# A two-model forward pass on one core: norms' roots behind the feed-forward products, attention halves split earlier, other POOL and load order

## The chip, the core and the metric

The kernel is one program on one core of a Trainium2 chip. The metric is device time in microseconds, the median of several runs. One further execution was recorded by the hardware profiler. Five engines work side by side: PE (matmul), DVE, ACT, POOL and SP, which here only issues DMAs.

## What is computed

Two blocks run in a row over 256 tokens of width 1024 (with 16 extra "meta" tokens in the second, so 272 columns there). The first has an mLSTM and sparse-attention layer and an HGRN2 layer, each behind an RMS norm. The second is a feed-forward, a mixer (stick-breaking attention beside an RWKV-7 recurrence), and a second feed-forward:

```python
def rms_norm_2(x, g):
    xf = x.astype(jnp.float32)
    y = xf * lax.rsqrt(jnp.mean(xf * xf, axis=-1, keepdims=True) + RMS_EPS)
    return (y * g.astype(jnp.float32)).astype(x.dtype)

def swiglu(h, w_gate, w_up, w_down):
    return (jax.nn.silu(h @ w_gate) * (h @ w_up)) @ w_down
...
        n = rms_norm_2(h, ffn1_norm[l])
        h = h + 0.5 * swiglu(n, ffn1_w_gate[l], ffn1_w_up[l], ffn1_w_down[l])
        n = rms_norm_2(h, mix_norm[l])
        proj = n @ w_in[l]
        ...
        h = h + jnp.concatenate([sb_out, rw_out], axis=-1) @ w_out[l]
        n = rms_norm_2(h, ffn2_norm[l])
        h = h + 0.5 * swiglu(n, ffn2_w_gate[l], ffn2_w_up[l], ffn2_w_down[l])
    return rms_norm_2(h, final_norm)[:, N_META:]
```

The root in `rms_norm_2` is one number per token, so it commutes with `h @ w_gate` and `h @ w_up`.

## The kernel before

**Layout.** Activations lie with features on the 128 partitions and tokens along the row: `xT` (the running sum), `hT` and `mixT` hold 8 tiles of 272 columns. All weights are cut into 253 units of 128x1024 numbers (512 KB) in one stream, in the order of use: `U_E` and `U_C` (first projection), `U_EO` (its output), `U_H` and `U_HO` (HGRN), `U_F1` (44 gate and up units in turn, then 22 down units), `U_P` and `U_PO` (mixer), `U_F2`. SP loads them into a ring of `SLOTS = 4`.

**Split products.** Every number of a large product is split into a rounded high half and the remainder. For a weight unit ACT writes `whi` (`high`, L1463) and POOL subtracts it from the ring to write `wlo` (`low`, L602); only then is the ring slot free for SP's next load. Activations get `aH` (ACT) and `aL` (DVE). PE makes three matmuls of each pair (`mm3`): high by high, high by low, low by high. A unit is 24 matmuls. Results go to four PSUM banks in turn (`MM_BANKS`); PE writes a bank again only when DVE or ACT has read the last result (`drained_v`, `drained_a`).

**Order.** Each engine runs its own program in the written order, with semaphores between them. ACT's `ahead(u)` waits until PE has used unit `u` and then makes the high half of unit `u + 4`. Where `ahead` stands behind another ACT step, a late input of that step delays the weights too. POOL's `lows(u0, u1)` makes the low halves of a range of units; between the ranges stand the decays of HGRN and `inverse_starts`, which fills `rGI` with identities and masks `rN` for the block inversion in RWKV.

**A norm.** `residual` (DVE, L1843) adds each of the 8 output tiles to `xT`. ACT squares a tile (`square`, L1402), DVE adds the first `SUMMED = 5` squares (L1834). PE sums over the partitions with a matrix of ones, ACT forms the root with Ln and Exp (`rstd`), DVE forms `hT` = x times weight times root (L1866), ACT rounds it to `aH`, DVE writes the remainder `aL` (L1872), and the first unit of the next projection can start. Meanwhile PE multiplies constants in `filler`.

**Feed-forward.** ACT takes the tanh of a gate bank (`fth`, L1673). DVE's `pair` makes `fhalf` from it and the gate (L2172), the product with the up bank (`fact`, L2177), and its two halves `fH` (L2180) and `fL` (L2182).

**The first layer's end.** `project_halves` multiplies the two halves of the output projection separately: attention's four tiles first (`mix_split` 1 to 4), the four memory heads' after them. All splits are written after the last memory head.

## Time and profile before

| | us |
|---|---|
| median of 3 runs | 1084.57 |
| the 3 runs | 1083.26 to 1085.09 |
| profiled execution, its own time | 1077.73 |
| span in its profile | 1075.9 |
| busy in it: PE, POOL, ACT, DVE | 992.6, 654.8, 535.2, 533.0 |
| mean granted TensorE clock | 0.974 of full speed |

Busy times are sums over the whole span. Which engine matters where is read from what PE waits for at one place, and from the time stamps around it. The profiled execution's own time is 6.8 us below the median of the three runs.

### The profile page before, as it was taken

The page shows a single profiled execution, that of the slowest core. Times are in us where ns is not written, and L with a number is a line of the kernel's source. Part 1 is how long each engine was busy: PE and PEld are TensorE (multiplying, and loading weights), DVE is VectorE, ACT ScalarE, POOL GpSimd, SP SyncE. Part 2 cuts the span into 40 slices and gives each one's busy share as a digit, 9 for nine tenths or more (in the row PEclk, how much of TensorE's full clock was granted, in tenths as well). Part 3 has the DMA queues.
Part 4 walks back from the last instruction along what each step waited for, and adds up shares of the span by engine and source line. Part 5 has one row for each costly group of instructions (what it writes and reads, how often), then busy time and mean ns, then how long its engine had stood idle before and what let it go on. Part 6 is the DMA issues. An engine that isn't in the chain of part 4 may idle for free.

```text
span 1075.9 us, 22914 instructions
## 1 busy us (share of the span) xinstructions
PE 992.6 (92%) x9068; PEld 944.6 (88%) x9068; DVE 533.0 (50%) x735; ACT 535.2 (50%) x765; POOL 654.8 (61%) x271
## 2 busy tenths in 40 slices
PE   5998999799799778999999999999999999999996
PEld 5987777698799767899999998999898879999996
DVE  4346424654410895586662003375274668777301
ACT  6565564556554445644444436676331554444441
POOL 2785234356689731698787775554620269888882
PEclk9998999999899899999999999999899999999999
DMA  8553122133355200455555553333300046555551
GB/s 321 195 169 106 60 79 98 59 118 128 127 177 177 79 1 2 149 187 177 177 171 177 176 176 124 117 117 115 99 4 4 23 136 207 188 192 179 192 177 41
DMA packets 38993, 139.79 MB, mean 130 GB/s; under 512 B 4224, under 2 KB 5504, under 8 KB 38784
## 3 DMA queue, kind: packets, MB, share of 16 engines
...
## 4 chain that ended last, share of the span: by engine, by line
PE 55%; issue 21%; POOL 12%; DVE 8%; ACT 2%; DMA 1%; SPq 0%; POOLq 0%; DVEq 0%; ACTq 0%
PE ps L667 55%; POOL wlo L602 11%; DVE qkl L1834 3%; DVE hA L2133 1%; DVE hT L1866 1%; ACT whi L1463 1%; ACT dif L1402 1%; DMA ring<-in_stream 1%; DVE sq L1834 0%; ACT rstd L1402 0%; POOL dif L626 0%; PE ps L1208 0%; DVE hA L1834 0%; DVE rGI L1834 0%; DVE aL L1872 0%
## 5 line engine op out<-in xcount | busy, mean ns | idle before, releaser
L602 POOL TENSOR_TENSOR wlo<-ring,whi 128x1024 fp32r<-128x1024 f32 x251 | 611.8, 2455 | 372.4 <-ACT whi L1463 371.5
L667 PE MATMUL ps<-aH,whi 128*128 128x256 f32 (+1 forms) x1528 | 444.0, 291 | 27.5 <-DVE aL L1834 11.8
L667 PE MATMUL ps<-aH,wlo 128*128 128x256 f32 (+1 forms) x1528 | 438.2, 287 | 0.0
L667 PE MATMUL ps<-aL,whi 128*128 128x256 f32 (+1 forms) x1528 | 437.8, 287 | 0.0
L1463 ACT ACTIVATE whi<-ring 128x1024 fp32r<-128x1024 f32 x253 | 266.3, 1058 | 122.9 <-PE ps L667 107.3
L667 PEld LDWEIGHTS ps<-aH,whi 128*128 128x128 f32 x1528 | 293.4, 192 | 35.3 <-POOL wlo L602 17.6
L667 PEld LDWEIGHTS ps<-aL,whi 128*128 128x128 f32 x1528 | 292.8, 192 | 0.5 <-issue 0.4
L667 PEld LDWEIGHTS ps<-aH,wlo 128*128 128x128 f32 x1528 | 293.1, 192 | 0.0
L667 PE MATMUL ps<-fH,wlo 128*128 128x272 f32 (+1 forms) x352 | 100.8, 286 | 0.0
L667 PE MATMUL ps<-fH,whi 128*128 128x272 f32 (+1 forms) x352 | 100.4, 285 | 0.0
L667 PE MATMUL ps<-fL,whi 128*128 128x272 f32 (+1 forms) x352 | 100.4, 285 | 0.0
L2182 DVE TENSOR_TENSOR fL<-fact,fH 128x272 f32 (+3 forms) x44 | 97.3, 2212 | 5.1
L1843 DVE SCALAR_TENSOR_TENSOR xT<-ps,xT 128x256 f32<-128x256 f32 (+1 forms) x40 | 17.1, 428 | 124.8 <-PE ps L667 124.1
L667 PEld LDWEIGHTS ps<-fH,whi 128*128 128x128 f32 x352 | 66.5, 189 | 0.0
L667 PEld LDWEIGHTS ps<-fL,whi 128*128 128x128 f32 x352 | 66.3, 188 | 0.0
L667 PEld LDWEIGHTS ps<-fH,wlo 128*128 128x128 f32 x352 | 66.2, 188 | 0.0
L1402 ACT ACTIVATE sq<-xT 128x256 f32<-128x256 f32 (+1 forms) x48 | 20.2, 421 | 69.7 <-DVE xT L1843 66.9
L1673 ACT ACTIVATE fth<-ps 128x272 f32<-128x272 f32 (+1 forms) x44 | 17.2, 391 | 60.8 <-PE ps L667 60.7
L667 PE MATMUL ps<-qkl 128*128 128x128 f32 x240 | 33.7, 307 | 13.2 <-DVE qkl L1834 13.2
L2180 DVE CAST fH<-fact 128x272 f32 (+3 forms) x44 | 42.4, 963 | 6.3 <-DVE fact L2177 3.4
L667 PEld LDWEIGHTS ps<-qkl 128*128 128x128 f32 x240 | 32.1, 219 | 14.7 <-DVE qkl L1834 14.7
L2177 DVE TENSOR_TENSOR fact<-fhalf,ps 128x272 f32<-128x272 f32 (+1 forms) x44 | 18.9, 430 | 37.2 <-PE ps L667 35.6
...
## 6 DMA issues: line engine op xcount, KB each, us to landing
ring<-in_stream SPq DMA_DIRECT2D x253, 512.0 KB, 3.3
...
out<-hT SPq DMA_DIRECT2D x1, 1024.0 KB, 4.6
...
```

Of the source, the lines that this page charges most:

```text
L602: nc.gpsimd.tensor_tensor(wlo[:, s, :], ring[:, s, :], whi[:, s, :].bitcast(F32), ALU.subtract).then_inc(S("w_split"), 1)
L667: return nc.tensor.matmul(out, lhsT, rhs, start=start, stop=stop, skip_group_check=True)
L1402: step(nc.scalar.activation(out, in_, f, **kw), sem)
L1463: nc.scalar.activation(whi[:, v % SLOTS, :], ring[:, v % SLOTS, :], ACT.Copy).then_inc(S("w_high"), 1)
L1673: nc.scalar.activation(fth[:, f4, c0:TT], ps[:, (g0 + 2 * f4) % MM_BANKS, 0:TT - c0], ACT.Tanh, scale=0.5).then_inc(S("ffn_th"), 1)
L1834: step(nc.vector.tensor_tensor(out, a, b, op), sem)
L1843: step(nc.vector.scalar_tensor_tensor(out=out, in0=a, scalar=s, in1=b, op0=op0, op1=op1), sem)
L1866: nc.vector.scalar_tensor_tensor(out=hT[:, j, c0:c0 + n], in0=xT[:, j, c0:c0 + n], scalar=V(w, j), in1=rstd[:, 0:n], op0=ALU.mult, op1=ALU ...
L2133: step(nc.vector.copy_predicated(v(out, 4), m.bitcast(U32), v(src, 4)), "lev_a")
L2177: nc.vector.tensor_tensor(prod, half, ps[:, (g0 + 2 * f4 + 1) % MM_BANKS, 0:TT - c0], ALU.mult).then_inc(S("drained_v"), 1)
L2180: nc.vector.tensor_copy(fH[:, f, c0:TT], prod).then_inc(S("ffn_hi"), 1)
L2182: nc.vector.tensor_tensor(fL[:, f, c0:TT], prod, fH[:, f, c0:TT].bitcast(F32), ALU.subtract).then_inc(S("ffn_split"), 1)
```

## The change

In words:

- **Late roots.** Before both feed-forwards (`LATE`), the input is split without the root: ACT writes `fxH` = x times norm weight, rounded, in front of the square; DVE writes `fxL` (`low_half`) from the sum itself. PE multiplies the first two units, and only then sums the squares. DVE multiplies each gate bank with the root before the tanh, and each of the 8 outputs of the down projection before adding it. The pair `fxH`, `fxL` takes the memory of `hT`, `mixT`.
- **Attention split earlier.** The four attention tiles are split by ACT behind unit 31 and by DVE behind unit 32 of the first projection, among the memory heads.
- **RWKV.** POOL fills the identities before the low halves of the four units `U_PO` to `U_PO` + 3, which wait for RWKV's third `r_u`. On PE three of the four key transposes stand before and within the products `r_u`.
- **Start.** DVE adds seven squares, PE multiplies two matrices for the first norm rather than four; ACT makes one high half before the root and one behind it; DVE's low halves follow, the second one within the norm.
- **End.** The output goes out in four pieces. `residual` adds its squares behind the sums, not ahead of them. `SUMMED` is a number per norm.

The diff, cut:

```diff
+LATE = ("ffn1", "ffn2")
+SUMMED = {"norm0": 7, "norm1": 5, "ffn1": 7, "mix": 5, "ffn2": 5, "final": 5}
+
+
+def sums_up_to(tag):
+
+    return sum(SUMMED[n] - 1 for n in NORMS[:NORMS.index(tag) + 1])
...
-        hT = sb("hT", [P, KT, TT])
-        mixT = sb("mixT", [P, KT, TT])
+        own = ExitStack()
+        hT = sb("hT", [P, KT, TT], at=own)
+        mixT = sb("mixT", [P, KT, TT], at=own)
+        own.close()
+        fxH = sb("fxH", [P, KT, TT], F32R)
+        fxL = sb("fxL", [P, KT, TT], F32R)
...
+        def acts(tag):
+
+            return (fxH[:], fxL[:]) if tag in ("ffn1", "ffn2") else (aH[:], aL[:])
...
-            sp.wait_ge(S("norm_h"), len(NORMS) * KT)
-            sp.dma_start(out_d, hT[:, :, TM:TT]).then_inc(S("out_done"), 16)
-            sp.wait_ge(S("out_done"), 16)
+            for k in range(0, KT, 2):
+                sp.wait_ge(S("norm_h"), (len(NORMS) - 1) * KT + k + 2)
+                sp.dma_start(out_d[:, k:k + 2, :], hT[:, k:k + 2, TM:TT]).then_inc(S("out_done"), 16)
+            sp.wait_ge(S("out_done"), 16 * KT // 2)
...
-            lows(U_HO + SLOTS, U_PO + SLOTS)
+            lows(U_HO + SLOTS, U_PO)
             inverse_starts()
-            lows(U_PO + SLOTS, N_UNITS)
+            pool.wait_ge(S("r_u"), 3)
+            lows(U_PO, N_UNITS)
...
                 i = NORMS.index(tag)
                 if i == 0:
                     pe.wait_ge(S("early_in"), 32)
-                else:
+                elif tag not in LATE:
                     filler(1)
-                pe.wait_ge(S("norm_sum"), (SUMMED - 1) * (i + 1))
-                mm(ps[:, 7, 0:n], C("ones"), sq[:, 0, 0:n], True, False)
-                for k in range(SUMMED, KT):
+                pe.wait_ge(S("norm_sum"), sums_up_to(tag))
+                m = mm(ps[:, 7, 0:n], C("ones"), sq[:, 0, 0:n], True, SUMMED[tag] == KT)
+                for k in range(SUMMED[tag], KT):
                     pe.wait_ge(S("norm_sq"), KT * i + k + 1)
                     m = mm(ps[:, 7, 0:n], C("ones"), sq[:, k, 0:n], False, k == KT - 1)
                 m.then_inc(S("norm_ss"), 1)
-                if i and tag != "final":
+                if tag in ("norm1", "mix"):
...
-                feature_pair(u0, g0, c0, ("norm_h", NORMS.index(tag) * KT))
+                feature_pair(u0, g0, c0, ("norm_h", NORMS.index(tag) * KT), tag)
+                norm(tag, TT - c0)
...
+                turned(6, key(0, 0)).then_inc(S("r_tok"), 1)
                 pe.wait_ge(S("r_wc"), 3)
                 for g, b in ((0, 0), (1, 4)):
                     pe.wait_ge(S("r_g"), level_count(last_level(g), g))
+                    if g == 1:
+                        turned(2, key(0, 1)).then_inc(S("r_tok"), 1)
+                        turned(3, key(1, 0)).then_inc(S("r_tok"), 1)
...
-                turned(2, key(0, 0)).then_inc(S("r_tok"), 1)
-                turned(3, key(0, 1)).then_inc(S("r_tok"), 1)
-                turned(6, key(1, 0)).then_inc(S("r_tok"), 1)
                 pe.wait_ge(S("r_tokb"), 1)
-                turned(2, key(1, 1)).then_inc(S("r_tok"), 1)
+                turned(6, key(1, 1)).then_inc(S("r_tok"), 1)
 
                 for c in range(4):
                     p, e = c // 2, c % 2
                     if e == 0:
-                        pe.wait_ge(S("r_tokb"), (4, 4)[p])
+                        pe.wait_ge(S("r_tokb"), (3, 4)[p])
...
+                if tag in LATE:
+                    func(acts(tag)[0][:, k, c0:TT], xT[:, k, c0:TT], ACT.Identity, "norm_hi", scale=V(tag, k))
                 func(sq[:, k, 0:n], xT[:, k, c0:c0 + n], ACT.Square, "norm_sq")
 
             def norm(tag, n):
                 act.wait_ge(S("norm_ss"), NORMS.index(tag) + 1)
                 func(rstd[:, 0:n], ps[:, 7, 0:n], ACT.Ln, scale=1.0 / D, bias=eps[:, 0:1])
                 func(rstd[:, 0:n], rstd[:, 0:n], ACT.Exp, "norm_rstd", scale=-0.5)
-                if tag != "final":
+                if tag == "norm0":
+                    high(1)
+                if tag in ("norm0", "norm1", "mix"):
                     for k in range(KT):
-                        act.wait_ge(S("norm_x"), NORMS.index(tag) * KT + k + 1)
+                        act.wait_ge(S("norm_x"), ("norm0", "norm1", "mix").index(tag) * KT + k + 1)
...
-                for u in range(2):
-                    high(u)
+                high(0)
                 act.wait_ge(S("setup"), 5)
-                act.wait_ge(S("early_in"), 32)
...
+                if tag in LATE:
+                    ahead(u0 + n_units - 1)
...
+                    if j == 31:
+                        act.wait_ge(S("att_o"), 8)
+                        for n in range(4):
+                            func(fxH[:, 4 + n, TM:TT], mixT[:, 4 + n, TM:TT], ACT.Copy, "mix_hi")
 
             def memory_out():
-                for n in range(4):
-                    act.wait_ge(S("mix_x"), n + 1)
-                    func(aH[:, 4 + n, TM:TT], mixT[:, 4 + n, TM:TT], ACT.Copy, "mix_hi")
...
-                    act.wait_ge(S("w_used"), it * 8 + (u0 + 2 * f4 + 1))
+                    ahead(u0 + 2 * f4, it)
+                    act.wait_ge(S("ffn_gate"), it * 4 + (first + f4 + 1))
...
+            def low(u):
+                dve.wait_ge(S("w_high"), u + 1)
+                tt(wlo[:, u, :], ring[:, u, :], whi[:, u, :].bitcast(F32), ALU.subtract, "w_split")
+
             def norm(tag, c0, n, w):
 
                 i = NORMS.index(tag) * KT
-                if tag == "norm0":
-                    for k in range(1, SUMMED):
+                first = tag == "norm0"
+                if first:
...
-                    for u in range(2):
-                        dve.wait_ge(S("w_high"), u + 1)
-                        tt(wlo[:, u, :], ring[:, u, :], whi[:, u, :].bitcast(F32), ALU.subtract, "w_split")
-                if tag == "norm0":
                     dve.wait_ge(S("early_in"), 32)
                     scaled_vectors()
+                    low(0)
...
+                lag = 1 if first else 2
...
+                    if first and j == 1:
+                        low(1)
+                    if split and j >= lag:
+                        k = j - lag
...
+                    if j == 32:
+                        for n in range(4):
+                            at = mixT[:, 4 + n, TM:TT]
+                            dve.wait_ge(S("mix_hi"), n + 1)
+                            tt(fxL[:, 4 + n, TM:TT], at, fxH[:, 4 + n, TM:TT].bitcast(F32), ALU.subtract, "mix_split")
...
             def residual(tag, g0, c0, scale=1.0):
-                for m in range(KT):
-                    if 2 <= m <= SUMMED:
-                        add_square(tag, m - 1, TT if tag in ("ffn1", "mix") else T)
-                    dve.wait_ge(S("w_used"), used_by(g0 + m))
-                    out = ps[:, (g0 + m // 2) % MM_BANKS, (m % 2) * T:(m % 2 + 1) * T] if tag in ("norm1", "ffn2") else \
-                        ps[:, (g0 + m) % MM_BANKS, 0:TT - c0]
-                    stt(xT[:, m, c0:TT], out, scale, xT[:, m, c0:TT], ALU.mult, ALU.add, "drained_v")
+                wide = TT if tag in ("ffn1", "mix") else T
+                for m in range(KT + 1):
+                    if m < KT:
+                        dve.wait_ge(S("w_used"), used_by(g0 + m))
+                        out = ps[:, (g0 + m // 2) % MM_BANKS, (m % 2) * T:(m % 2 + 1) * T] if tag in ("norm1", "ffn2") else \
+                            ps[:, (g0 + m) % MM_BANKS, 0:TT - c0]
+                        if tag in ("mix", "final"):
+                            tt(out, out, rstd[:, 0:TT - c0], ALU.mult)
+                        stt(xT[:, m, c0:TT], out, scale, xT[:, m, c0:TT], ALU.mult, ALU.add, "drained_v")
+                    if tag in LATE and m >= 1:
+                        low_half(tag, m - 1, wide)
+                    if 2 <= m <= SUMMED[tag]:
+                        add_square(tag, m - 1, wide)
+                if tag in LATE:
+                    dve.wait_ge(S("norm_rstd"), NORMS.index(tag) + 1)
+
+            def low_half(tag, k, n):
+
+                high, low = [t[:, k, TT - n:TT] for t in acts(tag)]
+                dve.wait_ge(S("norm_hi"), NORMS.index(tag) * KT + k + 1)
+                stt(low, xT[:, k, TT - n:TT], V(tag, k), high.bitcast(F32), ALU.mult, ALU.subtract, "norm_h")
...
+                    gate = ps[:, (g0 + 2 * f4) % MM_BANKS, 0:TT - c0]
+                    dve.wait_ge(S("w_used"), it * 8 + (u0 + 2 * f4 + 1))
+                    nc.vector.tensor_tensor(gate, gate, rstd[:, 0:TT - c0], ALU.mult).then_inc(S("ffn_gate"), 1)
                     dve.wait_ge(S("ffn_th"), it * 4 + (first + f4 + 1))
                     dve.wait_ge(S("drained_v"), it * 8 + (d0 + 2 * f4))
                     nc.vector.scalar_tensor_tensor(out=half, in0=fth[:, f4, c0:TT], scalar=1.0,
-                                                   in1=ps[:, (g0 + 2 * f4) % MM_BANKS, 0:TT - c0], op0=ALU.add,
+                                                   in1=gate, op0=ALU.add,
```

How it moves instructions, at three places. DVE, from the first residual of the HGRN output projection to the first feed-forward, before (`xT` is the sum, `sq` the squares):

```order
L1843 SCALAR_TENSOR_TENSOR xT<-ps,xT 128x256 [waits w_used,mix_split]
L1843 SCALAR_TENSOR_TENSOR xT<-ps,xT 128x256 [waits w_used,drained_v]
L1834 TENSOR_TENSOR sq<-sq 128x272 [waits norm_sq,drained_v]
L1843 SCALAR_TENSOR_TENSOR xT<-ps,xT 128x256 [waits w_used,norm_sum]
L1834 TENSOR_TENSOR sq<-sq 128x272 [waits norm_sq,drained_v]
L1843 SCALAR_TENSOR_TENSOR xT<-ps,xT 128x256 [waits w_used,norm_sum]
```

and in the changed kernel, the same place:

```order
L1867 SCALAR_TENSOR_TENSOR xT<-ps,xT 128x256 [waits w_used,mix_split]
L1867 SCALAR_TENSOR_TENSOR xT<-ps,xT 128x256 [waits w_used,drained_v]
L1867 SCALAR_TENSOR_TENSOR fxL<-xT,vec,fxH 128x272 [waits norm_hi,drained_v]
L1867 SCALAR_TENSOR_TENSOR xT<-ps,xT 128x256 [waits w_used,norm_h]
L1867 SCALAR_TENSOR_TENSOR fxL<-xT,vec,fxH 128x272 [waits norm_hi,drained_v]
L1858 TENSOR_TENSOR sq<-sq 128x272 [waits norm_sq,norm_h]
L1867 SCALAR_TENSOR_TENSOR xT<-ps,xT 128x256 [waits w_used,norm_sum]
```

Each later tile now has two instructions with two SBUF inputs (`fxL`, `sq`) behind its sum, where it had one.

ACT, at the end of the first projection, before (`hm` is the memory heads' output, `mixT` attention's, the `th` row the output gates' tanh):

```order
L1402 ACTIVATE rs<-hm 128x1024 [waits mlstm_h,mlstm_d]
L1402 ACTIVATE sq<-ps,vec 128x256 [waits w_used,ScalarE_once]
L1463 ACTIVATE whi<-ring 128x1024 [waits w_ready2,w_used,drained_a]
L1402 ACTIVATE aH<-mixT 128x256 [waits mix_x]
L1402 ACTIVATE aH<-mixT 128x256 [waits mix_x,mix_hi] x3
L1402 ACT_TABLE_LOAD [waits qk_ready]
L1402 ACTIVATE th<-sq 128x2048 [waits mix_hi]
```

and now:

```order
L1420 ACTIVATE fxH<-mixT 128x256 [waits att_o,mlstm_e]
L1420 ACTIVATE fxH<-mixT 128x256 [waits mix_hi] x3
L1420 ACTIVATE sq<-ps,vec 128x256 [waits w_used,mix_hi]
L1486 ACTIVATE whi<-ring 128x1024 [waits w_ready0,w_used,drained_a]
L1420 ACTIVATE mad<-ps 128x256 [waits mlstm_h,mlstm_o]
L1420 ACTIVATE mem<-ps 128x256 [waits mlstm_st,mlstm_s,mlstm_d]
```

The four copies stand two memory heads earlier, and the tanh follows directly on the last weight unit.

PE in RWKV, behind the last inversion level, before (`ps<-cst,sq` are the key transposes, `ps<-rWA,rGI` the products `r_u`):

```order
L667 MATMUL ps<-rWA,rGI 64x128 [waits r_g,r_wc]
L667 MATMUL ps<-rWA,rGI 64x128 x15
L667 MATMUL ps<-rWA,rGI 64x128 [waits r_g]
L667 MATMUL ps<-rWA,rGI 64x128 x17
L1208 MATMUL ps<-cst,sq 128x128 x12
L1208 MATMUL ps<-cst,sq 128x128 [waits r_tokb]
L1208 MATMUL ps<-cst,sq 128x128 x3
L667 MATMUL ps<-rWA,rN 64x64 [waits r_uc,r_tokb]
```

and now:

```order
L1227 MATMUL ps<-cst,sq 128x128 x4
L683 MATMUL ps<-rWA,rGI 64x128 [waits r_g,r_wc]
L683 MATMUL ps<-rWA,rGI 64x128 x15
L1227 MATMUL ps<-cst,sq 128x128 [waits r_g]
L1227 MATMUL ps<-cst,sq 128x128 x7
L683 MATMUL ps<-rWA,rGI 64x128 x18
L1227 MATMUL ps<-cst,sq 128x128 [waits r_tokb]
L1227 MATMUL ps<-cst,sq 128x128 x3
L683 MATMUL ps<-rWA,rN 64x64 [waits r_uc,r_tokb]
```

Twelve of the sixteen transposes moved ahead of the last products; one group of four stands between them and the state products.

## Rows read from the trace of the kernel before

**Rows 1.** The page: busy times, share of the span, instructions.

```profile
PE 992.6 (92%) x9068; PEld 944.6 (88%) x9068; DVE 533.0 (50%) x735; ACT 535.2 (50%) x765; POOL 654.8 (61%) x271
```

**Rows 2.** The chain in order of time: start us, us, what; both feed-forwards.

```profile
447.62 202.93 PE ps L667 x1594
...
876.14 190.37 PE ps L667 x1594
```

**Rows 3.** Timeline of PE, start (first two), first layer's end, FFN 1 entrance.

```profile
7.56 3.78 PE L667 MATMUL ps<-sq,cst 128*128 128x256 f32 x8 [7.56 <-DMA cst<-in_cst]
15.89 0.55 PE L667 MATMUL ps<-aH,whi 128*128 128x256 f32 x1 [4.55 <-DVE aL L1872]
214.50 0.55 PE L667 MATMUL ps<-aH,whi 128*128 128x256 f32 x1 [7.52 <-DVE aL L1834]
...
441.92 0.89 PE L667 MATMUL ps<-cst 128*128 128x432 f32 x2
447.62 0.36 PE L667 MATMUL ps<-aH,whi 128*128 128x272 f32 x1 [0.81 <-DVE aL L1872]
```

**Rows 4.** Timeline there, then windows (PE, PEld, DVE, ACT, POOL, PEclk, DMA).

```profile
211.56 1.74 ACT L1402 ACTIVATE aH<-mixT 128x256 fp32r<-128x256 f32 x4
211.99 3.74 DVE L1834 TENSOR_TENSOR aL<-mixT,aH 128x256 fp32r<-128x256 f32 x4 [3.08 <-ACT aH L1402]
225.19 0.42 DVE L1834 TENSOR_TENSOR aL<-ps,aH 128x256 fp32r<-128x256 f32 x1 [1.04 <-ACT aH L1402]
240.55 0.89 PE L667 MATMUL ps<-cst 128*128 128x432 f32 x2
...
214.50:220.00 5.50, 5.50 (x29) 5.39 (x30) 4.43 (x6) 4.14 (x4) 0.00 (x0) 0.68 0.29 98
```

**Rows 5.** DVE beside POOL: FFN 2's loop, then the entrance of FFN 1.

```profile
928.16 1.89 DVE L2180 CAST fH<-fact 128x256 f32 x1 [0.16 <-DVE fact L2177]
927.50 9.76 POOL L602 TENSOR_TENSOR wlo<-ring,whi 128x1024 fp32r<-128x1024 f32 x4 [2.07 <-ACT whi L1463]
435.70 1.54 DVE L1834 TENSOR_TENSOR sq<-sq 128x272 f32<-128x272 f32 x1 [0.57 <-ACT sq L1402]
426.85 17.33 POOL L602 TENSOR_TENSOR wlo<-ring,whi 128x1024 fp32r<-128x1024 f32 x7 [33.76 <-ACT whi L1463]
```

**Rows 6.** Groups of DVE by form: busy us, mean ns, idle before.

```profile
L2182 DVE TENSOR_TENSOR fL<-fact,fH 128x256 f32 x20 | 49.3, 2464 | 2.5
L1872 DVE TENSOR_TENSOR aL<-hT,aH 128x272 fp32r<-128x272 f32 x16 | 6.6, 435 | 0.0
L2177 DVE TENSOR_TENSOR fact<-fhalf,ps 128x256 f32<-128x256 f32 x22 | 9.3, 422 | 13.2 <-PE ps L667 12.1
```

**Rows 7.** Timeline at the entrance of FFN 2.

```profile
868.13 0.89 PE L667 MATMUL ps<-cst 128*128 128x432 f32 x2
872.10 1.15 PE L667 MATMUL ps<-sq,cst 128*128 128x256 f32 x4 [0.70 <-ACT sq L1402]
```

**Rows 8.** Timeline of RWKV's start, then windows.

```profile
763.81 0.38 ACT L1402 ACTIVATE mixT<-ps 128x272 f32<-128x272 f32 x1
770.45 2.13 POOL L639 COPY rGI<-cst 128x1088 f32<-128x1088 f32 x2
773.61 5.60 PE L667 MATMUL ps<-hT,sq 64*64 64x128 f32 x64 [2.44 <-DVE rA L1834]
...
776.00:778.00 2.00, 2.00 (x30) 2.00 (x24) 1.77 (x3) 0.00 (x0) 1.99 (x1) 0.50 0.01 4
```

**Rows 9.** Timeline: state products in RWKV, the end; the page's DMA issue.

```profile
821.82 0.34 PE L667 MATMUL ps<-rWA,rN 64*64 64x64 f32 x4 [1.52 <-DVE rN L2318]
848.66 2.40 POOL L602 TENSOR_TENSOR wlo<-ring,whi 128x1024 fp32r<-128x1024 f32 x1 [46.54 <-ACT whi L1463]
1067.62 3.26 DVE L1866 SCALAR_TENSOR_TENSOR hT<-xT,vec,rstd 128x256 f32<-128x256 f32 x8 [3.05 <-ACT rstd L1402]
...
out<-hT SPq DMA_DIRECT2D x1, 1024.0 KB, 4.6
```

32 lines of the change are left out of this document (13 added, 19 removed).

## The prediction, made before the changed kernel was run

> **What bounds the kernel now.** I read the busy times of the page first: PE is busy 992.6 of 1075.9 us, POOL 654.8, ACT and DVE 535 each [rows 1]. So no other engine bounds the whole, and the part to be won is the 83 us in which PE stands or multiplies for nothing. The chain of waits says where PE cannot be helped: 1594 matmuls of the first feed-forward in 202.93 us (0.127 each, so a unit of 24 is 3.06 and a gate and up pair 6.1), and as many of the second in 190.37 us (0.119, 2.87 and 5.7) [rows 2]. The change takes no weight unit away. Then I read PE's timeline for gaps at the places that the diff touches: the start (first product at 15.89), 7.52 us at the first layer's end, 5.7 us from the last product before FFN 1 (441.92) to its first (447.62) [rows 3], 8.0 us before FFN 2 (868.13 to 876.14) [rows 2, 7], 2.44 us and half the clock at RWKV's start [rows 8], 1.52 us in its state products, and the end behind the last norm [rows 9]. That is about 27 us in reach. Last I read what DVE and POOL do to each other, since the change gives DVE more work at these places.
>
> DVE instructions that read PSUM cost the same with POOL at work or not: `fact` takes 422 ns in the mean of 22 [rows 6]. Those with two SBUF inputs don't: a remainder of 256 columns takes 0.435 when POOL rests, 2.464 in the mean in the feed-forward, the square's sum 1.54 instead of 0.43 while POOL runs seven low halves in a row (17.33, so 2.48 each), and even the cast `fH` 1.89 beside four of them [rows 5, 6]. They wait until POOL's running instruction is through.
>
> The Trainium skill has this as a rule (SBUF — State Buffer, section "Who interferes with whom"): DVE and GpSimd share one port pair as an exclusive lock, which a DVE instruction takes when both its inputs lie in SBUF, and the later one fully blocks. This case's trace agrees, 2.464 against 0.435. The rule speaks against this change, since `fxL` is made from `xT` and `fxH`, both in SBUF, at the moment when POOL is busiest. Without it the two entrances would be worth 11.1 us, with it the 5.4 below.
>
> **The change part by part.** Gains in us, against the profiled execution (1077.73, of which the span is 1075.9).
>
> *Start, 0.7.* Eight records in 3.78 are four matmuls at 0.94 [rows 3]; two go, but DVE adds two more squares (0.43 each), so the root comes about 1.1 earlier. PE's first product could gain 1.3, but the second high half now stands behind the root, and the later loads hang on it. Bounds 0 and 1.3; I take the middle.
>
> *First layer's end, 4.5.* ACT's four copies (1.74) and DVE's four remainders (3.74) leave the path [rows 4]; PE's 7.52 go almost whole, so attention's half starts at about 207.0, not 214.50. It takes 96 matmuls, some 11 us. But the memory heads' half hangs on its own chain (tanh, Ln, Exp, first `aL` at 225.19 [rows 4]), which gains only the 1.74 of the copies and about 1 that ACT waited for PE's sums: first `aL` at 222.4, last at 225. PE then waits 4 us between the halves, and ends at 235.5 instead of 240.55 [rows 4]. The slow clock behind the gap (0.68 in the window from 214.50 [rows 4]) goes or comes back behind the new one, so 4.5. Lower bound 3 (the clock falls again), upper 8 (the whole gap and the clock).
>
> *Entrance of FFN 1, 3.0.* The root leaves the path; two matmuls over the squares (two take 1.15 with the tail of the second, or 0.46 and 0.46 when others follow them [rows 7]) follow the pair: nothing waiting, 5.7 - 0.9 = 4.8. What is late next is DVE. Behind the last output it has a sum (0.42), two remainders and a square's sum, each of the latter 1.5 with POOL busy [rows 5]: done at 442.2 + 0.4 + 3.0 = 445.6. The first unit touches the last tile 2.5 us after its start, so PE starts at 443.2, and ACT, which now has two steps per tile and the highs of weights behind them, adds about 0.4: PE waits 1.7 instead of 5.7, less 0.9: 3.0. Bounds 4.6 (remainders at 0.435) and 0.8 (at 2.464).
>
> *Entrance of FFN 2, 2.4.* Here four matmuls stand behind the pair, 1.6. When the last output is done (868.13) DVE has three tiles left: 868.6 + 3 x (0.45 + 1.5) = 874.4, less 2.5: PE starts at 872.0, a wait of 3.9. 8.0 - 3.9 - 1.6 = 2.5, I say 2.4. Bounds 6.3 (no wait) and 0 (remainders at 2.464 give 874.8, and the 1.6 eat the rest).
>
> *Roots on outputs, -1.0.* Each down output gets a product of 0.42 in front of its sum, by `fact`'s row [rows 6]. For seven tiles PE's next output covers it; for the last it lies on the path to the norm, twice: 0.9 to 1.0.
>
> *The loop of gate and up, -0.5.* DVE gets 0.42 per pair and ACT's tanh must wait for it. DVE's row per pair is now 0.42 (gate) + 0.42 (`fhalf`, of `fact`'s kind) + 0.42 (`fact`) + 1.9 and 2.46 (`fH` and `fL` beside POOL), 5.6, with the gaps between them 5.8 [rows 5, 6], with a pair at 5.7 on PE [rows 2]. That is even; the four banks give some slack, so a little at each end. Bounds 0 and -4.
>
> *RWKV fills, 5.2.* The fills start at 770.45, behind four low halves, though the last attention output is written at 764.2 [rows 8]. Written first they end before PE needs them (`rA` hangs on them), so the 2.44 goes, and with it the clock of 0.50 in the rows that follow [rows 8], where 64 matmuls take 5.60: at the other level 3.0. 2.44 + 2.6 = 5.0, and a little issue time behind it. Bounds 4.5 and 5.5. The delayed four low halves (9.8 on POOL) now wait for RWKV's third `r_u`, which stands ahead of the state products at 821.82; POOL's next low half comes at 848.66, behind 46.54 us of rest, when PE has used the first of these units [rows 9]. Some 20 us hide 9.8, so they cost nothing; without that cover they would cost 9.8.
>
> *Key transposes, 1.5.* The wait of 1.52 before the state products [rows 9] goes, since three of the four transposes and DVE's copies of them no longer stand behind the products `r_u`. Bounds 0 (the last transpose is still there to wait for) and 1.5.
>
> *Output in four pieces, 2.0.* `hT` is written in 3.26, then one transfer takes 4.6 for 1024 KB [rows 9]. Now three quarters run beside the norm and only 256 KB behind it. Even at a fixed part of half the row, 4.6 becomes about 2.9; at none 1.2. Bounds 1.5 and 2.2, since the pieces are themselves made over 3.26.
>
> Sum: 0.7 + 4.5 + 3.0 + 2.4 - 1.0 - 0.5 + 5.2 + 1.5 + 2.0 = 17.8. The profiled execution goes to 1059.9; the median lay 6.8 above it, and 1084.57 - 18 = 1066.5.
>
> **Rivals.** *A, the forecast* (contended entrances, loop even): 1066.5, chance 0.50.
>
> *B, DVE keeps up.* ACT and DVE find POOL idle between low halves, the entrances give 4.6 and 6.3 and the first layer's end 7: 17.8 + 1.7 + 3.9 + 2.5, 26 us: 1058. For it: POOL is busy only 61% of the span [rows 1]. Against: sums of 1.54 in the row at FFN 1 [rows 5]. 0.22.
>
> *C, DVE eats both entrances.* Remainder and square both cost 2.464, and the loop loses 4: 17.8 - 2.2 - 2.4 - 3.5 = 9.7, with the first layer's end at 3 another 1.5 off: about 1076. For it: the mean of 2.464 [rows 6]. Against: at the entrances the rows show 1.54. 0.18.
>
> *D, slower: the loop becomes bound by DVE.* If `fH`, `fL` and the gate's product leave the rhythm of POOL so that a pair needs three of its slots (3 x 2.45 = 7.35 against 5.7), each pair loses 1.65, 22 pairs 36, less the banks' slack of about 8: 28 in one feed-forward, more than the 17.8. It decides from 0.8 us a pair over both feed-forwards (44 pairs less 17 slack). For it: DVE's 5.8 already stand against the pair's 5.7. Against: `fact` waits 12.1 us in all for PE over 22 tiles [rows 6], so DVE isn't behind now. 1084.57 - 17.8 + 28 = 1095. 0.07.
>
> *E, nothing left*: C and half of D together cancel, 0.03.
>
> **How the numbers follow.** The predicted time is A's, whose own range is 1063 to 1070 (the halves between its terms' bounds). A to C span 1056 to 1077 and leave D, E and the tails out, 0.2. A measurement of this kernel tells about 0.2% (2.2 us) from no change. Faster by over 0.2% are A, B and C: 0.90; within it E: 0.03; slower D: 0.07.
>
> **What the profile of the changed kernel would show.** First layer's end: attention's half of PE starts near 207 and a new wait of 3 to 5 us stands behind it. FFN 1 and 2: PE waits for `fxL` 1 to 2 and 3 to 4 us; with under 1 us B holds, with 5 or over C. Remainders `fxL` have a mean of 1 to 1.6 us. FFN 2's loop takes 190 us again within 2; 200 or more is D, and the row that ends PE's waits there is `fact` or `fL`. RWKV: no half clock behind the fills, and POOL's fills before 768. The state products no longer wait 1.5. The last DMA lands under 3 us from its issue. The prediction is wrong if the clock falls in a new place, or if `ahead`, now standing behind two more steps of ACT, makes PE wait for a weight unit that nobody counted.

## The result: slower, 1108.94 us, and the profile after

| | before | after |
|---|---|---|
| median, us | 1084.83 (4 runs, 1083.26 to 1086.63) | 1108.94 (4 runs, 1106.69 to 1111.07) |
| span of the profiled execution | 1075.9 | 1107.2 |

The ratio of after to before is 1.0221, with a 95% interval of 1.0196 to 1.0247. The forecast was 1066.5, in a range of 1056 to 1077. The two profiled executions differ by more than the medians, 31.3 against 24.1 us: the one of the kernel before is 7.1 under its median (at a granted clock of 0.974, where nearly all other runs of that kernel have 0.963 to 0.971), the one of the changed kernel (1108.98) is at its median.

The page of the changed kernel, busy times and then the chain that ended last by engine:

```profile
PE 995.0 (90%) x9044; PEld 942.3 (85%) x9044; DVE 622.8 (56%) x783; ACT 532.9 (48%) x765; POOL 653.0 (59%) x271
...
PE 28%; DVE 28%; issue 26%; POOL 13%; ACT 3%; DVEq 1%; DMA 0%; POOLq 0%; SPq 0%; ACTq 0%
```

PE is as busy as in [rows 1] in a span that is 31 us longer, and DVE has 90 us more. The table of PE's waits (engine, line, waited for: us in total, times, longest) begins with a row that the kernel before doesn't have:

```profile
PE ps L683 <- DVE fhalf L2221: 33.1, 32, 1.4
```

`fhalf` is what frees a gate's bank. The groups of DVE by form say which instructions grew (busy us, mean ns, idle before); `fL` x20 and 272 columns wide is FFN 1's, 256 columns FFN 2's, which had 2464 ns before [rows 6]:

```profile
L2231 DVE TENSOR_TENSOR fL<-fact,fH 128x272 f32 x20 | 48.5, 2426 | 2.5
L2231 DVE TENSOR_TENSOR fL<-fact,fH 128x256 f32 x20 | 48.2, 2411 | 2.5
L2229 DVE CAST fH<-fact 128x272 f32 x20 | 45.7, 2287 | 3.7 <-DVE fact L2226 1.7
L2229 DVE CAST fH<-fact 128x256 f32 x20 | 40.3, 2014 | 3.3 <-DVE fact L2226 3.3
```

`fL` waited for a low half before as well. `fH` did so in part of its turns only: over both feed-forwards its mean was 963 ns, and is 1994.

PE's timeline gives the ends of the stages: the end of the first layer, both entrances, the ends of both feed-forwards.

```profile
237.44 0.89 PE L683 MATMUL ps<-cst 128*128 128x432 f32 x2
440.00 0.36 PE L683 MATMUL ps<-fxH,whi 128*128 128x272 f32 x1 [1.76 <-POOL wlo L617]
...
665.34 0.89 PE L683 MATMUL ps<-cst 128*128 128x432 f32 x2
671.04 0.36 PE L683 MATMUL ps<-aH,whi 128*128 128x272 f32 x1 [0.81 <-DVE aL L1901]
883.54 0.35 PE L683 MATMUL ps<-fxH,whi 128*128 128x256 f32 x1 [4.18 <-POOL wlo L617]
...
1097.36 0.89 PE L683 MATMUL ps<-cst 128*128 128x432 f32 x2
```

With the same rows of before ([rows 2, 3, 4, 7]; the feed-forwards there end at 647.82 and 1063.88, the mixer starts at 653.53) the 31.3 us come apart:

| stretch of PE | before | after | difference |
|---|---|---|---|
| to the first layer's end | 240.55 | 237.44 | -3.1 |
| HGRN layer | 201.4 | 200.8 | -0.6 |
| wait before FFN 1 | 5.7 | 1.8 | -3.9 |
| FFN 1 | 200.2 | 225.3 | **+25.1** |
| norm before the mixer | 5.7 | 5.7 | 0 |
| mixer and RWKV | 214.6 | 208.3 | -6.3 |
| wait before FFN 2 | 8.0 | 4.2 | -3.8 |
| FFN 2 | 187.7 | 213.8 | **+26.1** |
| last norm and output | 12.0 | 9.8 | -2.2 |

Everything outside the two feed-forwards is 19.9 us shorter. The prediction's terms for the same stretches come to 22.0, with the norms' matmuls (0.9 and 1.6) counted in the feed-forwards, where they now stand. The two feed-forwards lose 51.2, where these matmuls, the roots on outputs and the loop were to cost 4.0. DVE's timeline in FFN 1 shows one turn of the loop (start, us, instruction, idle before):

```profile
464.93 0.45 DVE L2218 TENSOR_TENSOR ps<-ps,rstd 128x272 f32<-128x272 f32 x1
465.92 0.44 DVE L2221 SCALAR_TENSOR_TENSOR fhalf<-fth,ps 128x272 f32<-128x272 f32 x1 [0.54 <-ACT fth L1698]
466.48 0.44 DVE L2226 TENSOR_TENSOR fact<-fhalf,ps 128x272 f32<-128x272 f32 x1
467.06 2.41 DVE L2229 CAST fH<-fact 128x272 f32 x1
469.60 2.44 DVE L2231 TENSOR_TENSOR fL<-fact,fH 128x272 f32 x1
472.15 0.45 DVE L2218 TENSOR_TENSOR ps<-ps,rstd 128x272 f32<-128x272 f32 x1
...
465.49 0.40 ACT L1698 ACTIVATE fth<-ps 128x272 f32<-128x272 f32 x1 [5.03 <-DVE ps L2218]
465.78 2.00 ACT L1486 ACTIVATE whi<-ring 128x1024 fp32r<-128x1024 f32 x2
466.91 4.82 POOL L617 TENSOR_TENSOR wlo<-ring,whi 128x1024 fp32r<-128x1024 f32 x2 [2.40 <-ACT whi L1486]
```

It is a ring through three engines, a chain of waits that comes back to where it began. DVE's product of gate and root (464.93) stands behind the last pair's `fL`; ACT has waited 5.03 us for it, and behind its tanh stand two high halves; POOL has stood idle 2.40 us for these, and starts its low half at 466.91, just ahead of `fH` at 467.06. So `fH` waits for the whole of one low half and `fL` for the whole of the next: 7.22 us a turn, against 6.1 for a pair on PE [rows 2]. The same timelines in FFN 2 show how the ring closes (the two rows of POOL in the middle are from narrow windows, so that single starts can be read; the `DVEq` rows are from the chain of waits, time of DVE's sequencer at the head of its loop of four pairs, L2235):

```profile
908.70 0.30 DVE L2229 CAST fH<-fact 128x256 f32 x1 [0.16 <-DVE fact L2226]
909.12 2.42 DVE L2231 TENSOR_TENSOR fL<-fact,fH 128x256 f32 x1
913.75 0.29 DVE L2229 CAST fH<-fact 128x256 f32 x1 [0.16 <-DVE fact L2226]
916.99 0.43 DVE L2218 TENSOR_TENSOR ps<-ps,rstd 128x256 f32<-128x256 f32 x1 [0.40 <-DVE fL L2231]
919.17 2.33 DVE L2229 CAST fH<-fact 128x256 f32 x1 [0.16 <-DVE fact L2226]
921.62 2.42 DVE L2231 TENSOR_TENSOR fL<-fact,fH 128x256 f32 x1
...
916.70 0.06 DVEq L2235
916.88 0.06 DVEq L2235
...
913.56 1.28 ACT L1486 ACT_TABLE_LOAD   x1
917.54 0.39 ACT L1698 ACTIVATE fth<-ps 128x256 f32<-128x256 f32 x1 [1.62 <-DVE ps L2218]
...
913.77 5.08 POOL L617 TENSOR_TENSOR wlo<-ring,whi 128x1024 fp32r<-128x1024 f32 x2
918.95 4.81 POOL L617 TENSOR_TENSOR wlo<-ring,whi 128x1024 fp32r<-128x1024 f32 x2
...
901.11 22.64 POOL L617 TENSOR_TENSOR wlo<-ring,whi 128x1024 fp32r<-128x1024 f32 x9
926.12 2.40 POOL L617 TENSOR_TENSOR wlo<-ring,whi 128x1024 fp32r<-128x1024 f32 x1 [2.36 <-ACT whi L1486]
```

At first POOL runs its low halves without a break (nine in 22.64). `fH` starts 0.01 to 0.02 us ahead of a low half (913.75 against 913.77), takes 0.30, only `fL` waits, and DVE turns in 5.05, catching up with PE. The next turn is 0.37 longer, most of it at the head of DVE's own loop (0.40 idle before the product, where the turns before leave about 0.12). So the next `fH` starts at 919.17, 0.22 us behind a low half (918.95), and waits for it: 2.33. Now ACT's tanh and high halves come too late for POOL, which runs dry at 923.75, and from then on each turn takes 7.06 to 7.54. ACT's table load (1.28) isn't in this chain: it is over at 914.84, and the next tanh has waited 1.62 for DVE's product. In FFN 1 the second pair's `fH` already waits 2.52 (it starts at 459.74, a low half at 459.71). These are readings of one trace; no run shifted the starts alone.

### The profile page after: what moved, and what is told of

The parts are those of the page before. It is cut to its first block, busy times and chain, and to the rows that moved or that the text cites. A ratio compares the mean times of both kernels' runs of the same rounds, so it can differ in the third digit from the quotient of the medians.

```text
span 1107.2 us, 23000 instructions
## 1 busy us (share of the span) xinstructions
PE 995.0 (90%) x9044; PEld 942.3 (85%) x9044; DVE 622.8 (56%) x783; ACT 532.9 (48%) x765; POOL 653.0 (59%) x271
## 4 chain that ended last, share of the span: by engine, by line
PE 28%; DVE 28%; issue 26%; POOL 13%; ACT 3%; DVEq 1%; DMA 0%; POOLq 0%; SPq 0%; ACTq 0%
PE ps L683 28%; POOL wlo L617 12%; DVE fL L2231 10%; DVE fH L2229 8%; DVE qkl L1858 2%; DVE ps L2218 2%; DVE fact L2226 2%; DVE fhalf L2221 2%; ACT fth L1698 2%; DVE hA L2179 1%; DVE hT L1893 1%; ACT whi L1486 1%; DMA ring<-in_stream 0%; POOL rN L662 0%; ACT rstd L1420 0%
## 5 line engine op out<-in xcount | busy, mean ns | idle before, releaser
L1486 ACT ACTIVATE whi<-ring 128x1024 fp32r<-128x1024 f32 x253 | 262.6, 1056 | 56.2 <-PE ps L683 38.8
L683 PE MATMUL ps<-fxH,whi 128*128 128x256 f32 (+1 forms) x768 | 226.2, 294 | 40.1 <-DVE fhalf L2221 31.1
L683 PE MATMUL ps<-aH,whi 128*128 128x256 f32 (+1 forms) x760 | 225.8, 297 | 19.3 <-POOL wlo L617 9.3
L683 PE MATMUL ps<-fxH,wlo 128*128 128x256 f32 (+1 forms) x768 | 220.7, 287 | 0.0
L683 PE MATMUL ps<-aH,wlo 128*128 128x256 f32 (+1 forms) x760 | 220.2, 290 | 0.0
L683 PE MATMUL ps<-aL,whi 128*128 128x256 f32 (+1 forms) x760 | 220.2, 290 | 0.0
L683 PE MATMUL ps<-fxL,whi 128*128 128x256 f32 (+1 forms) x768 | 220.0, 286 | 0.0
L683 PEld LDWEIGHTS ps<-fxH,whi 128*128 128x128 f32 x768 | 146.9, 191 | 49.6 <-DVE fhalf L2221 32.5
L683 PEld LDWEIGHTS ps<-aH,whi 128*128 128x128 f32 x760 | 149.0, 196 | 26.3 <-POOL wlo L617 10.6
L683 PEld LDWEIGHTS ps<-fxH,wlo 128*128 128x128 f32 x768 | 146.9, 191 | 0.0
L683 PEld LDWEIGHTS ps<-fxL,whi 128*128 128x128 f32 x768 | 146.8, 191 | 0.1
## 6 DMA issues: line engine op xcount, KB each, us to landing
cst<-in_cst SPq DMA_DIRECT2D x1, 1325.0 KB, 12.5
```

Of the source, the lines that this page charges most:

```text
L683: return nc.tensor.matmul(out, lhsT, rhs, start=start, stop=stop, skip_group_check=True)
L1486: nc.scalar.activation(whi[:, v % SLOTS, :], ring[:, v % SLOTS, :], ACT.Copy).then_inc(S("w_high"), 1)
```

## The experiments

Two theories stood against each other. **Ring**: it is the order, the product behind `fL` and ACT's high halves behind the product, that makes POOL and DVE meet at the worst moment. **Load**: DVE has too much to do when `fH` and `fL` each wait for POOL, whatever the order. The kernel before, run beside them, had medians of 1084.4 to 1085.4.

### e1: the tanh doesn't wait for DVE

The part of the computation left out is the root inside the tanh.

```diff
-                    act.wait_ge(S("ffn_gate"), it * 4 + (first + f4 + 1))
+                    act.wait_ge(S("w_used"), it * 8 + (u0 + 2 * f4 + 1))
...
+                    dve.wait_ge(S("ffn_th"), it * 4 + (first + f4 + 1))
                     dve.wait_ge(S("w_used"), it * 8 + (u0 + 2 * f4 + 1))
                     nc.vector.tensor_tensor(gate, gate, rstd[:, 0:TT - c0], ALU.mult).then_inc(S("ffn_gate"), 1)
-                    dve.wait_ge(S("ffn_th"), it * 4 + (first + f4 + 1))
+                    dve.wait_ge(S("ffn_gate"), it * 4 + (first + f4 + 1))
```

> The changed kernel, but ACT takes the tanh of the raw gate bank as soon as PE has written it, and DVE makes its product with the root behind that tanh. The tanh lacks the root, so this part of the computation is left out; DVE has the same instructions as in the changed kernel. Theory R (a ring: the product stands behind the last remainder fL on DVE, the tanh and the up unit's high half behind the product on ACT, the low halves behind that on POOL, and fH and fL behind the low halves): the ring is cut, both feed-forwards fall from 228 and 214 us to within 5 us of 203 and 190, the time is about 1060 to 1068. Theory L (load: DVE simply has too much to do once each of fH and fL waits for a low half, whatever the order): a pair stays at 7.0 to 7.3 us, the time is 1100 to 1109.

Measured: 1064.3 (ratio to before 0.9797, 0.9778 to 0.9816). DVE has the same instructions as in the changed kernel, and its groups by form are

```profile
L2232 DVE TENSOR_TENSOR fL<-fact,fH 128x256 f32 x20 | 34.6, 1728 | 2.5
L2230 DVE CAST fH<-fact 128x256 f32 x20 | 9.4, 468 | 3.3 <-DVE fact L2227 3.3
```

`fH` is down from 2014 to 468 ns. 44.6 us came from the order alone. Theory load falls: DVE still does every instruction, and the time is gone.

### e2: no product at all

The root on the gate is left out, with the product and ACT's wait for it.

> The changed kernel without DVE's product of the gate with the root and without ACT's wait for it; the root on the gate is left out, 44 instructions of 0.45 us less. Theory R: the loop is PE-bound again, 203 and 190 us, the time about 1058 to 1062. Theory L: 0.45 us of 7.3 per pair go, plus nothing else: 7.3 becomes 6.8, the time 1087 to 1090. If it stays at 1105 or more, the gate's product isn't the cause, and something else in the feed-forward is (the input's other tiles, the norm inside it).

Measured: 1062.21 (0.979, 0.9772 to 0.9808). Against e1 the 44 products themselves are worth 2 us at most, within the spread of the two (1061.65 to 1065.55); what they did to the order was worth 45.

### e3: `fact` in PSUM

```diff
-                    half, prod = fhalf[:, c0:TT], fact[:, f4 % 2, c0:TT]
+                    half, prod = fhalf[:, c0:TT], ps[:, (g0 + 2 * f4 + 1) % MM_BANKS, 0:TT - c0]
...
-                    nc.vector.tensor_tensor(prod, half, ps[:, (g0 + 2 * f4 + 1) % MM_BANKS, 0:TT - c0],
-                                            ALU.mult).then_inc(S("drained_v"), 1)
-                    dve.wait_ge(S("drained_v"), it * 8 + (d0 + 2 * f4 + 2))
+                    nc.vector.tensor_tensor(prod, half, prod, ALU.mult).then_inc(S("ffn_prod"), 1)
+                    dve.wait_ge(S("ffn_prod"), it * 4 + (first + f4 + 1))
```

`fL` then signals `drained_v`, and PE's down projection waits for that.

> The changed kernel, but fact is written back over the up unit's bank in PSUM, so fH is a cast from PSUM and fL has one SBUF input; the bank comes free behind fL. Everything is computed. Both theories R and L hold that fH (mean 1994 ns) and fL (2428 ns) are long only because they wait for POOL's low half: then both come to 0.45 us, a pair is PE-bound again, and the time is about 1058 to 1064. The rival to both, that the two are long by themselves or that POOL waits for them in turn so that nothing is won: the means stay over 1.5 us and the time over 1095.

Measured: 1062.95 (0.9794, 0.9778 to 0.9811). The groups of DVE:

```profile
L2228 DVE CAST fH<-ps 128x272 f32 x20 | 8.8, 442 | 2.9 <-DVE ps L2226 0.2
L2230 DVE TENSOR_TENSOR fL<-ps,fH 128x272 f32 x20 | 8.8, 441 | 2.4
```

With `fact` in PSUM (`fH` then has no input in SBUF, `fL` one) neither waits for POOL at all: 441 for 2426, 442 for 2287. The product still stands behind `fL` here and the tanh behind the product; the ring is whole but has lost its two long arms.

### e4: the next pair's product between `fH` and `fL`

```diff
+                def root(it, f4):
+                    gate = ps[:, (g0 + 2 * f4) % MM_BANKS, 0:TT - c0]
+                    dve.wait_ge(S("w_used"), it * 8 + (u0 + 2 * f4 + 1))
+                    nc.vector.tensor_tensor(gate, gate, rstd[:, 0:TT - c0], ALU.mult).then_inc(S("ffn_gate"), 1)
...
-                    dve.wait_ge(S("w_used"), it * 8 + (u0 + 2 * f4 + 1))
-                    nc.vector.tensor_tensor(gate, gate, rstd[:, 0:TT - c0], ALU.mult).then_inc(S("ffn_gate"), 1)
+                    dve.wait_ge(S("ffn_gate"), it * 4 + (first + f4 + 1))
...
                     nc.vector.tensor_copy(fH[:, f, c0:TT], prod).then_inc(S("ffn_hi"), 1)
+                    if f4 + 1 < 4 and not (isinstance(it, int) and f4 + 1 >= FT % 4):
+                        root(it, f4 + 1)
+                    elif f4 + 1 == 4:
+                        root(it + 1, 0)
                     dve.wait_ge(S("ffn_hi"), it * 4 + (first + f4 + 1))
...
+                root(0, 0)
```

> The changed kernel with the next pair's product of gate and root written between fH and fL of this pair, not behind fL. Everything is computed, and DVE has the same instructions. Theory R: the tanh and the high half behind it come 2.5 us sooner, the ring is shorter than PE's 6.1 and 5.7 us; time 1060 to 1070. Theory L: the order on DVE changes nothing, 1100 to 1109.

Measured: 1063.01 (0.9791, 0.9774 to 0.9807), everything computed. PE's timeline:

```profile
643.15 0.89 PE L683 MATMUL ps<-cst 128*128 128x432 f32 x2
860.07 0.36 PE L683 MATMUL ps<-fxH,whi 128*128 128x256 f32 x1 [4.11 <-POOL wlo L617]
1051.61 0.89 PE L683 MATMUL ps<-cst 128*128 128x432 f32 x2
```

FFN 1 takes 643.15 - 440.15 = 203.0, FFN 2 191.5: 22.3 less than in the changed kernel, each. Moving one instruction of 0.45 us over one of 2.4 gives back 45.9 us. Both waits are now shorter than in the kernel before: `fH` has means of 589 and 708 ns in the two feed-forwards (934 and 1084 before), `fL` of 955 and 1265 (2092 and 2464).

### e6: both cures

> The product early and fact in PSUM, together. Theory R: either alone already puts the loop behind PE, so the second adds nothing: within 1.5 us of 1063. If some loss from DVE were left in either, up to 4 us less.

Measured: 1062.58 (0.9811, 0.9772 to 0.985). The second cure adds nothing: no loss that either would cure is left in the loop.

### e7: the up unit's high half ahead of the tanh

```diff
                     ahead(u0 + 2 * f4, it)
+                    ahead(u0 + 2 * f4 + 1, it)
                     act.wait_ge(S("ffn_gate"), it * 4 + (first + f4 + 1))
```

(and its old place behind the tanh is gone).

> The changed kernel, its product still behind fL on DVE, but ACT makes the up unit's high half before the tanh, so low halves no longer hang on DVE. Theory R, with POOL as an arm of the ring: POOL's low halves go at PE's pace again and no longer start just as fH does; fH comes down to about 1 us, a pair is 5.9 to 6.1 us, the time 1062 to 1075. If the arm through ACT's high halves and POOL does not matter, and the tanh's round trip behind fL alone makes the 7.3: fH stays at 2 us and the time at 1100 or more.

Measured: 1077.86 (0.9949, 0.9929 to 0.997), 31 us better than the changed kernel but 2.9 above the expected window. The edit didn't cut the arm as I had thought: ACT works in order, so both high halves still stand behind the tanh of the pair before. DVE's timeline in FFN 1 has both kinds of turn side by side: three of 7.0 to 7.3, then a short one of 3.7 to 4.0; in FFN 2 it is so at first, and from the middle on the turns are of 5.0 to 6.7. `fH` has a mean of 2016 ns in FFN 1 and of 1164 in FFN 2. So the time at which ACT's high halves are made matters too; how much hangs on this arm alone it can't say.

### e5: roots in front of the products again

The rest of the change stays, and the loop's product is gone with the late roots.

> The changed kernel with the roots of both feed-forwards back in front of the products, as before the change; start, attention split, RWKV, transposes, output pieces and the order of squares stay. Everything is computed. If the ring through the gate's product is the whole of the loss, both feed-forwards take 203 and 190 us, and the time is the changed kernel with its product early (1063.0) plus what late roots win at the two entrances (3.9 and 3.8 read from the traces, less 2.6 for the norms' matmuls and 0.9 for the roots on outputs, so about 4): 1065 to 1069. If the late roots win nothing, 1061 to 1064.

Measured: 1067.01 (0.9856, 0.9817 to 0.9895). Against e4 the late roots, cured, win 4.0 us; against e6, which ran beside e5, 4.4.

### e12: a late root at FFN 1 only

The kernel of e3, but FFN 2 has its root in front of the products again.

> Fact in PSUM (1062.95), with the late root at FFN 1 only; FFN 2 has its root in front of the products again, as before the change. Everything is computed. The traces of the runs with the root early and late say where late roots win: from the last product before FFN 1 to its end 207.2 against 204.8 us, from the last product before FFN 2 to its end 195.55 against 195.65. So only FFN 1's should count: 1062 to 1064, no change. If the late root at FFN 2 was worth its planned 2.4 us in the runs, 1065 to 1066.

Measured: 1062.33 (0.9798, 0.9781 to 0.9815). Against e3 at 1062.95 that is no difference beyond the spread of either (1060.74 to 1063.55): at FFN 2 the late root wins nothing that can be seen.

### e8: POOL's fills behind the four low halves again, on e4

```diff
-            lows(U_HO + SLOTS, U_PO)
+            lows(U_HO + SLOTS, U_PO + SLOTS)
             inverse_starts()
-            pool.wait_ge(S("r_u"), 3)
-            lows(U_PO, N_UNITS)
+            lows(U_PO + SLOTS, N_UNITS)
```

> The kernel with the product early (1063.0), with POOL's order in RWKV as before the change: four low halves ahead of the fills. The prediction's 5.2 us for this part: 1068.2; the traces' offset between the mixer's start and the second inversion level says 5.9: 1068.9. If the gain came from elsewhere between them, 1063.

Measured: 1067.28, so the part is worth 4.3. Its windows show the slow clock back (the columns of [rows 4]):

```profile
768.00:772.00 4.00, 4.00 (x41) 3.67 (x34) 2.97 (x5) 0.00 (x0) 2.33 (x1) 0.50 0.00 0
```

From the mixer's norm to the second inversion level e8 takes 142.2 and e4 136.3, so 6.0 are won; from there to FFN 2 it takes 79.4 and e4 80.7, so 1.2 are lost again.

### e11: the delayed low halves at once behind the inversion's masks, on e4

POOL's wait for the third `r_u` is taken out.

> The kernel with the product early, without POOL's wait for the third r_u: the four delayed low halves follow POOL's last mask product at once, during the last inversion levels, where they meet other DVE work. The late place costs 1.25 us by the traces (stretch from the last fills' level to FFN 2: 80.67 against 79.44 with the low halves ahead of the fills). If the cost lies in what DVE does behind r_u: 1061.8. If DVE loses as much in the inversion: 1063, or more, up to 1066, since there it stands on the path at every level.

Measured: 1066.77, 3.8 more than e4. DVE's and POOL's timelines show why:

```profile
789.96 2.73 DVE L1857 TENSOR_TENSOR rGI<-rGI,ps 128x1024 f32<-128x1024 f32 x3
792.72 1.89 DVE L1911 CAST aH<-mixT 128x256 fp32r<-128x256 f32 x1
794.64 2.46 DVE L1857 TENSOR_TENSOR aL<-mixT,aH 128x256 fp32r<-128x256 f32 x1
797.13 2.32 DVE L1861 TENSOR_SCALAR pK<-pr,vec 128x256 f32<-128x256 f32 x1
...
789.59 9.71 POOL L617 TENSOR_TENSOR wlo<-ring,whi 128x1024 fp32r<-128x1024 f32 x4
```

Three small instructions of 0.3 to 0.45 us wait for POOL, and the inversion's `rGI` stand behind them. So the change's wait for the third `r_u` earns its place.

### e9: attention's split back at the end, on e4

> The kernel with the product early, with attention's four tiles split behind the last memory head again, as before the change. The prediction's 4.5 us for this part: 1067.5. The traces show the first layer's end 3.1 us earlier in all, the start included, so if the start gives nothing by then: 1066.1. The rival, that the memory heads' chain sets this end either way and only the 1.74 us of ACT's copies count: 1064.8.

Measured: 1070.04. The five runs fall into two groups: two of 1066.19 at granted clocks of 0.976 and 0.978, and three of 1070.04 to 1071.51 at 0.970 to 0.972. The trace is of one of the first. In it the first layer ends at 242.53, 5.0 later than e4's 237.52, and 2.8 of it are left at the end of FFN 2. So the part is worth 2.8 to 2.9 at the higher clock, as the trace and its execution agree (1066.19 against e4's 1063.26), and 7 or more where the clock is lower; none of e4's four runs is under 0.977. Where the clock is lost then, no trace shows.

### e10: squares behind the remainders at FFN 2, on e4

> The kernel with the product early, where DVE adds the squares of the norm before FFN 2 behind all its sums and remainders, no longer between them. In the profile one such addition takes 2.62 us there, with ACT idle for 3.64 behind it and PE waiting 4.1 for the second unit's low half. If this addition is what holds the chain: the wait falls by 2 to 3 us, and the time to 1060 to 1061. If the remainders then wait for POOL in its place, or PE waits for the norm's sums behind the pair: 1062 to 1064.

Measured: 1063.72, no gain. PE's timeline:

```profile
859.26 0.35 PE L683 MATMUL ps<-fxH,whi 128*128 128x256 f32 x1 [2.20 <-DVE xT L1867]
868.25 3.53 PE L683 MATMUL ps<-sq,cst 128*128 128x256 f32 x8 [2.62 <-DVE sq L1858]
```

The wait ahead of the pair fell from 4.11 to 2.20, and PE waits 2.62 for the same squares behind it, at the lower clock besides (the eight records take 3.53, where they take 1.89 behind the last norm of the changed kernel).

## Why the prediction was wrong, step by step

**The loop of gate and up** is the step that failed. It priced the new product at 0.42 us of DVE's time, found "about 5.8" against 5.7, called that even, and gave -0.5 with bounds of 0 and -4; by e4 the order alone cost 44.6 (22.3 in each feed-forward). It took the row's 1.9 for `fH` as a price, where it was one sample of a wait (the mean before was 1084 ns in FFN 2, and is 2014). The step asked how much DVE does in a turn, not what now stands behind the product: ACT's tanh and, in order behind it, the high halves on which POOL's next start hangs. e1 has the same load and none of the loss. The text named `ahead` "behind two more steps of ACT" as a thing that would make it wrong, but priced it nowhere. PE's waits end at `fhalf` (33.1 us), the step that frees the bank, not at `fact` or `fL` as rival D's sign said. Rival D had the right rhythm, three slots of POOL (7.35; measured 7.22) and the wrong odds, 0.07. It argued that each of `fH`, `fL` and the product takes a slot; the product doesn't wait for POOL (0.45), the third slot is tanh and high half. It also counted one feed-forward, 28 us; both have it, 22.3 each by e4. "`fact` waits 12.1 us for PE, so DVE isn't behind now" spoke of the loop while DVE follows PE. The loop can also lock at 7.2, and in FFN 2's trace 0.4 us of lateness went ahead of that. With the ring out (e4) the feed-forwards take 2.8 and 3.8 us more than before; the norms' matmuls and the clock (below) come to about 2.6 and 3.3 of that, so without the ring -0.5 for the loop would have been about right.

**Contention at the entrances: the sizes right, the releaser wrong.** PE waits 1.76 before FFN 1 (forecast 1.7) and 4.18 before FFN 2 (3.9); the remainders `fxL` take 1.87 and 1.23 us in the mean, where 1.5 was counted. But what releases PE is the second unit's low half, not `fxL`. POOL waits for ACT's high half, which stands in order behind `fxH` and a square, and these wait for a sum that DVE makes only behind a blocked remainder or square's sum (2.62 us for one before FFN 2 in e4). That is the weight unit behind "two more steps of ACT" that the prediction gave as a sign of being wrong. The sum that hit both waits followed another path, so how close it came is in part luck; when the order of the squares changed (e10), the wait became 2.20. The chain before FFN 2, in e4:

```profile
852.22 2.62 DVE L1858 TENSOR_TENSOR sq<-sq 128x256 f32<-128x256 f32 x1
855.39 0.51 ACT L1420 ACTIVATE fxH<-xT,vec 128x256 fp32r<-128x256 f32 x1 [3.58 <-DVE xT L1867]
857.51 2.35 POOL L617 TENSOR_TENSOR wlo<-ring,whi 128x1024 fp32r<-128x1024 f32 x1 [2.96 <-ACT whi L1486]
```

**Their net value: too high.** Forecast were 3.0 and 2.4 less 1.0 for both roots on outputs, 4.4 in all (3.9 with the loop's -0.5). From the last product before FFN 1 to its end it is 205.9 before and 204.8 in e4; for FFN 2, 195.75 and 195.65. That is 1.1 and 0.1. The norm's matmuls behind the pair were counted; the clock was not, though the text named it as a sign of being wrong. e4's windows (columns as in [rows 4]) right behind the two entrances:

```profile
440.10:445.00 4.90, 4.85 (x26) 4.88 (x27) 4.79 (x6) 2.19 (x4) 4.25 (x2) 0.65 0.56 161
860.00:865.00 5.00, 4.93 (x29) 4.96 (x30) 4.33 (x7) 2.70 (x6) 2.38 (x1) 0.66 0.50 147
```

Before, the filler ran in these gaps and the windows of 9 us behind them stand at 1.00. A third of 5 us is 1.7 us, twice: an estimate of the loss. Against e5, which keeps the new count and order of squares, the late roots come to 4.0 by the medians. The traces give 2.4 at FFN 1 and -0.1 at FFN 2 (207.2 and 195.55 in e5 from the last product to the end), and the two profiled executions differ by 1.8, so some 2 us of the 4.0 can't be placed.

**First layer's end: right in kind, 1.4 too much.** Attention's half begins at 207.20, as forecast (207.0), and PE then waits three times for the memory heads' `fxL`, 2.5 us in all, as PE's timeline shows for two of them:

```profile
223.09 0.36 PE L683 MATMUL ps<-fxH,whi 128*128 128x256 f32 x1 [1.84 <-DVE fxL L1858]
224.97 0.39 PE L683 MATMUL ps<-fxH,whi 128*128 128x256 f32 x1 [0.37 <-DVE fxL L1858]
```

The second half starts 0.7 later than the 222.4 forecast, and the clock in the window from 221.20 to 237.40 is 0.89, where the last 12.5 us before stood at 1.00. That the clock falls again behind the new wait was the lower bound of 3. Forecast 4.5, measured 3.1.

**Start: 0, not 0.7.** The first product is 1.94 us earlier (13.95), but 72 us on nothing is left of it (`kct` at 86.01, before 85.84); the granted clock from 60 to 90 us is 0.94, and was 1.00.

**RWKV fills: 5.2 forecast, 6.0 won and 1.2 given back.** That the delayed low halves "cost nothing" was wrong by that 1.2. Part of it is in one stretch: PE is busy 7.30 of 8 us there (e4, 814 to 822) and 7.00 of 7 in e8 (818 to 825), with one idle piece of 0.55 for nothing that the profile shows, while the DMA share is 0.58 against 0.02. The cause stays open; no run separated it.

**Key transposes: 1.3 of 1.5.** From the last inversion level (811.24 before, 803.57 in e8) to the last product ahead of FFN 2 (868.13, 859.18) it takes 56.9 before and 55.6 in e8, which has the transposes' new order and not the low halves.

**Output: 2.2 of 2.0.** From the last norm's first filler to the end 12.0 became 9.8. The page's DMA issues of the changed kernel, beside the 4.6 of [rows 9]:

```profile
out<-hT SPq DMA_DIRECT2D x4, 256.0 KB, 2.4
```

The subtraction `fL` with two inputs in SBUF takes 2.43 us in the mean of the changed kernel's 44, and with one 0.42 to 0.44 (e3), as the rule of the Trainium skill has it that the prediction weighed (SBUF — State Buffer, section "Who interferes with whom"); the trace agrees. As the prediction put it the rule speaks of two SBUF inputs, and `fH` has one and waited too. It says who waits, not how often; that is set by the order of three engines.

**The step from trace to median.** With the ring out of the way the forecast of 1066.5 would have stood 3.5 us above the measurement (1063.01), but by two errors that nearly cancel. In the traces e4 wins 14.5 us (1061.4 against 1075.9), where the parts were to give 17.8; in the medians it wins 21.8. The forecast took the 6.8 by which the profiled execution of the kernel before lay under its median as fixed, and for the changed kernels it isn't there: the changed kernel and e4 (1063.26) were profiled at their medians. So in most of its executions the kernel before loses some 7 us that its trace doesn't show, at granted clocks of 0.963 to 0.971 against the trace's 0.974, and the change takes them away. e9 brings back 4 to 5 us of that kind in three of five runs, so attention's split has a share in it; the rest isn't placed.

Two small slips in the prediction's working change nothing: the uncontended entrances add to 10.9 by its own bounds, not 11.1, and the remainder of 0.435 is of 272 columns, not 256.
